# The end of an expert loop: last two passes written out, last expert's rows added on chip, norm by tile

## What is computed

```python
def moe(xn, ...):
    logits = xn @ w_router + b_router
    top_v, top_i = lax.top_k(logits, 4); gates = softmax(top_v)
    # for each expert e, on the rows routed to it:
    hdn = x @ w1[e] + b1[e]
    gate = min(hdn[:, :1024], 7); lin = clip(hdn[:, 1024:], -7, 7)
    y = (gate * sigmoid(1.702 * gate) * (lin + 1)) @ w2[e] + b2[e]
    # each row of y times its gate is added to its token's row
h = h + moe(rmsnorm(h))
out = rmsnorm(h, norm_final_g)
```

## Time and profile before

| | |
|---|---|
| time, median of 3 runs | 2095.84 us (2093.32 to 2096.25) |
| span of the profiled execution | 2096.6 us |
| PE matmul busy | 1978.0 us, 94%, 9222 matmuls |
| DVE busy | 1593.4 us, 76% |
| ACT busy | 1225.3 us, 58% |
| HBM traffic | 260 GB/s over the span |

### The profile page before, as it was taken

The page is one execution under the profiler, slowest core; times in us unless marked ns, Lnnn a source line. Parts: engine busy times, 40 slices in busy tenths (PEclk is TensorE's granted clock), DMA queues, the critical chain, the costliest instruction groups (busy, mean ns, idle before and its releaser), DMA issues. The chain is left out here.

```text
span 2096.6 us, 25970 instructions
## 1 busy us (share of the span) xinstructions
PE 1978.0 (94%) x9222; PEld 1600.6 (76%) x9222; DVE 1593.4 (76%) x1534; ACT 1225.3 (58%) x1058; POOL 245.6 (12%) x177
## 2 busy tenths in 40 slices
PE   6889899999999999999999999999999999999992
PEld 4778677677777888778888888888888888888881
DVE  4753637878775236589999999999999999999983
ACT  5553535446344213357777777777777777777763
POOL 0000031442612000100010010000101000000000
PEclk9899899999999999889999999999999999999996
DMA  5222424442535935489999999999999999999982
GB/s 133 67 77 71 159 73 140 131 140 82 171 97 174 338 99 169 149 320 370 362 374 362 375 363 362 375 367 373 362 375 357 375 360 371 367 358 376 366 298 88
DMA packets 212049, 541.08 MB, mean 258 GB/s; under 512 B 16438, under 2 KB 131544, under 8 KB 175064
## 3 DMA queue, kind: packets, MB, share of 16 engines
q1 hardware_dynamic: 204600, 518.54, 68.0%
q0 software_dynamic: 7392, 21.77, 4.4%
HBM read 512.87 MB, written 31.59 MB: 260 GB/s over the span
## 5 line engine op out<-in xcount | busy, mean ns | idle before, releaser
L1678 DVE TENSOR_TENSOR w_low<-ring_b,w_high 128x2048 fp32r<-128x2048 f32 x192 | 435.8, 2287 | 40.5 <-ACT w_high L1672 40.1
L1678 DVE TENSOR_TENSOR w_low<-ring_a,w_high 128x2048 fp32r<-128x2048 f32 x192 | 435.4, 2286 | 40.3 <-ACT w_high L1672 40.0
L1672 ACT ACTIVATE w_high<-ring_b 128x2048 fp32r<-128x2048 f32 x192 | 368.3, 1919 | 156.7 <-PE ps L1779 109.4
L1672 ACT ACTIVATE w_high<-ring_a 128x2048 fp32r<-128x2048 f32 x192 | 368.1, 1918 | 156.6 <-PE ps L1779 115.0
L1779 PE MATMUL ps<-w_high,rows_high 128*128 128x512 f32 x1024 | 403.7, 394 | 0.2
L1779 PE MATMUL ps<-w_high,rows_low 128*128 128x512 f32 x1024 | 400.4, 391 | 0.0
L1779 PE MATMUL ps<-w_low,rows_high 128*128 128x512 f32 x1024 | 399.5, 390 | 0.0
L1779 PEld LDWEIGHTS ps<-w_high,rows_high 128*128 128x128 f32 x1024 | 193.0, 189 | 42.9 <-DVE w_low L1678 3.5
L1779 PEld LDWEIGHTS ps<-w_high,rows_low 128*128 128x128 f32 x1024 | 192.6, 188 | 41.0
L1779 PEld LDWEIGHTS ps<-w_low,rows_high 128*128 128x128 f32 x1024 | 193.1, 189 | 39.8
L1843 PE MATMUL ps<-w_high,act_high 128*128 128x512 f32 x512 | 207.0, 404 | 15.2 <-DVE w_low L1678 7.6
(11 more groups left out here) (342 smaller groups left out, 2875.2 us busy)
## 6 DMA issues: line engine op xcount, KB each, us to landing
ring_a<-in_w SPq DMA_DIRECT2D x192, 1024.0 KB, 7.8
ring_b<-in_w SPq DMA_DIRECT2D x192, 1024.0 KB, 7.8
unit_raw<-in_w_in SPq DMA_DIRECT2D x80, 512.0 KB, 4.4
temps<-cum_rows SPq DMA_DIRECT2D x16, 1024.0 KB, 7.1
unit_raw<-in_w_up_ssd SPq DMA_DIRECT2D x16, 512.0 KB, 7.9
ssd_out_T<-y_high SPq DMA_DIRECT2D x4, 1024.0 KB, 6.6
ssd_out_T<-y_low SPq DMA_DIRECT2D x4, 1024.0 KB, 6.8
ssd_high<-ssd_out_T SPq DMA_DIRECT2D x4, 1024.0 KB, 11.3
```

Source lines behind the costliest of these rows:

```text
L1672: nc.scalar.activation(w_hi[:, split_at(it, j)], slot(at, 1)[:, 0, :], ACT.Copy).then_inc(w_hi_ok, 1)
L1678: nc.vector.tensor_tensor(w_lo[:, split_at(it, j)], slot(at, 1)[:, 0, :], w_hi[:, split_at(it, j)].bitcast(F32), ALU.subtract).then_inc(w_ ...
```

## The change

The loop ends two passes earlier. Pass 30 is written out with `more=False`: it doesn't prepare later experts (no index matmuls, no `tokens_dve`, no `slots_dve`). Pass 31 is written out as `last_pe`, `last_act`, `last_dve`. It has no row transposes for a next expert. PE instead transposes the 0/1 matrix of expert 31 into bank 6 and ACT copies it to `sel_T`. The transposes of expert 31's activations come before the fourth unit of expert 30's down product. The activations are kept in the buffers of the rows (`rows_hi`, `rows_lo`), and the down product of expert 31 goes to banks 0 and 1.

Expert 31 is not scattered. Its product, times the gate, is split into high and low parts (`y2_hi`, `y2_lo`), and PE multiplies them by `sel_T` into a pair of banks for each tile of tokens. For tiles 0 and 3 PE also adds the residual by a product with the identity; for tiles 1 and 2 DVE adds it. SP reloads the residual once the scatter-add of expert 30 has landed, in the same block of the program; the second block is gone. The norm goes tile by tile: ACT squares and takes the root with scale and bias (a first root on a constant stands ahead of it), DVE takes the reciprocal and does one pass that multiplies by it and by the gain, SP stores each tile. The trip count drops two small DVE instructions, and ACT and POOL one register load each. The cut diff:

```diff
-        def rows_pe(pe, it, odd):
+        def rows_pe(pe, it, odd, more=True):
             pe.wait_ge(xe_in, it * 16 + 16)
-            pe.wait_ge(ix_ok, it * 3 + 6)
+            pe.wait_ge(ix_ok, it * 3 + (6 if more else 3))
...
-                if k == 2:
+                if k == 2 and more:
                     if not is_first(it):
...
-            tokens_dve(v, it + 2)
-            slots_dve(v, it + 3)
+            if more:
+                tokens_dve(v, it + 2)
+                slots_dve(v, it + 3)
...
+        BY_PE = (0, 3)
+        def rows_at(t):
+            return (2 + 2 * t) % 8
...
+        def last_pe(pe, it, end):
+            up_pe(pe, it, 1, False)
+            pe.wait_ge(s_oh, it + 3)
+            pe.wait_ge(a_lo_ok, it)
+            for t in range(NT):
+                last = nc.tensor.transpose(ps[0:CAP, 6, tokens(t)], sel[:, t, :].bitcast(F32), ident[:])
+            last.then_inc(sT_ps, 1)
+            pe.wait_ge(ye_ok, it - 1)
+            for u in range(DOWN):
+                if u == DOWN - 1:
+                    pe.wait_ge(glu_ok, it + 1)
+                    pe.wait_ge(sT_ok, sT_ok0 + 1)
+                    for c in range(NK):
+                        last = nc.tensor.transpose(ps[:, 6 + c // 4, (c % 4) * CAP:(c % 4 + 1) * CAP], l_w[0:CAP, c * P:(c + 1) * P], ident[0:CAP, 0:CAP])
+                    last.then_inc(aT_tp, 1)
+                down_tile(pe, it, UP + u, u, 4, acts_hi, acts_lo).then_inc(w_used, 1)
+            pe.wait_ge(acts2_lo, acts2_lo0 + 1)
+            for u in range(DOWN):
+                down_tile(pe, end, u, u, 0, rows_hi, rows_lo).then_inc(w_used, 1)
+        def last_act(act, it, end, last):
+            for j in range(3):
+                high_act(act, it, 1, j)
+            acts_act(act, it - 1)
+            down_act(act, it - 1, TILES, it * 16 - 32)
+            for j in range(3, UP + 3):
+                high_act(act, it, 1, j)
+            act.wait_ge(h_out, 16 * NT)
+            act.wait_ge(sT_ps, sT_ps0 + 1)
+            nc.scalar.activation(sel_T[0:CAP, :], ps[0:CAP, 6, :], ACT.Copy).then_inc(sT_ok, 1)
+            silu_act(act, it)
+            high_act(act, it, 1, UP + 3)
+            high_act(act, end, 0, 0)
+            act.wait_ge(aT_tp, it + 1)
+            nc.scalar.activation(slots_in(x_hi), eighths(6), ACT.Copy, scale=1.0 / ALPHA).then_inc(acts2_hi, 1)
+            high_act(act, end, 0, 1)
+            down_act(act, it, TILES, last * 16)
+            high_act(act, end, 0, 2)
+            high_act(act, end, 0, 3)
+        def last_dve(v, it, end):
+            for j in range(3):
+                low_dve(v, it, 1, j)
+            acts_dve(v, it - 1)
+            for j in range(3, 6):
+                low_dve(v, it, 1, j)
+            places_dve(v, it - 1)
+            nc.vector.tensor_copy(gate_z2[0:CAP, :], gate_f[0:CAP, bass.ds(it % 4, 1)]).then_inc(last_gate, 1)
+            nc.vector.memset(eps_c, EPS).then_inc(last_gate, 1)
+            v.wait_ge(ix_ps, it + 1)
+            nc.vector.tensor_tensor(sel, iota_r[:, bass.ds(it // NE * CAP, CAP)].unsqueeze(1).broadcast_to([P, NT, CAP]),
+                                    rank_m[:, bass.ds(it % NE * NT, NT)].unsqueeze(2).broadcast_to([P, NT, CAP]), ALU.is_equal).then_inc(s_oh, 1)
+            for j in range(6, UP + 2):
+                low_dve(v, it, 1, j)
+            gate_dve(v, it)
+            low_dve(v, it, 1, UP + 2)
+            linear_dve(v, it)
+            low_dve(v, it, 1, UP + 3)
+            glu_dve(v, it)
+            low_dve(v, end, 0, 0)
+            v.wait_ge(acts2_hi, acts2_hi0 + 1)
+            nc.vector.scalar_tensor_tensor(slots_in(x_lo), eighths(6), 1.0 / ALPHA,
+                                           slots_in(x_hi).bitcast(F32), ALU.mult, ALU.subtract).then_inc(acts2_lo, 1)
+            for j in range(1, DOWN):
+                low_dve(v, end, 0, j)
...
+        def finish_pe(pe):
+            def rows(t, j, part):
+                halves = y2_hi, y2_lo
+                return nc.tensor.matmul(ps[:, rows_at(t) + j, :], sel_T[0:CAP, tokens(t)], halves[part][0:CAP, j * 512:(j + 1) * 512],
+                                        start=part == 0 and t not in BY_PE, stop=part == 1, skip_group_check=True)
+            def residual(t):
+                pe.wait_ge(r_in[t], 48)
+                for j in range(2):
+                    nc.tensor.matmul(ps[:, rows_at(t) + j, :], ident[:], fin[:, t, j * 512:(j + 1) * 512], start=True, stop=False, skip_group_check=True)
+            residual(0)
+            for j in range(2):
+                pe.wait_ge(y2_hi_ok, y2_hi0 + j + 1)
+                for t in range(NT - 1):
+                    rows(t, j, 0)
+            pe.wait_ge(y2_lo_ok, y2_lo0 + 2)
+            for t in range(NT - 1):
+                rows(t, 0, 1)
+                rows(t, 1, 1).then_inc(fin_ps, 1)
+            residual(3)
+            for j in range(2):
+                rows(3, j, 0)
+                last = rows(3, j, 1)
+            last.then_inc(fin_ps, 1)
+        def finish_act(act, end):
+            act.wait_ge(last_gate, last_gate0 + 2)
+            nc.scalar.activation(stat[:, 60:61], eps_c, ACT.Sqrt).then_inc(fin_rt, 1)
+            act.wait_ge(w_used, tile_no(end, DOWN - 1) + 1)
+            for j in range(2):
+                cols = slice(j * 512, (j + 1) * 512)
+                nc.scalar.activation(y2_hi[0:CAP, cols], ps[0:CAP, j, :], ACT.Copy, scale=gate_z2[0:CAP, :]).then_inc(y2_hi_ok, 1)
+            for t in range(NT):
+                if t in BY_PE:
+                    act.wait_ge(fin_ps, fin_ps0 + t + 1)
+                    src = ps[:, rows_at(t):rows_at(t) + 2, :]
+                else:
+                    act.wait_ge(fin_ok, fin_ok0 + t)
+                    src = fin[:, t, :].rearrange("p (a b) -> p a b", a=2)
+                if t:
+                    act.wait_ge(fin_sq, fin_sq0 + t)
+                nc.scalar.activation(fin_junk.rearrange("p (a b) -> p a b", a=2), src, ACT.Square, accum_out=stat[:, t:t + 1]).then_inc(fin_sq, 1)
+                act.wait_ge(fin_sq, fin_sq0 + t + 1)
+                nc.scalar.activation(stat[:, 8 + t:9 + t], stat[:, t:t + 1], ACT.Sqrt, scale=1.0 / D, bias=eps_c).then_inc(fin_rt, 1)
+        def finish_dve(v):
+            v.wait_ge(h_out, 16 * NT)
+            v.wait_ge(gf_in, 48)
+            for j in range(2):
+                cols = slice(j * 512, (j + 1) * 512)
+                v.wait_ge(y2_hi_ok, y2_hi0 + j + 1)
+                nc.vector.scalar_tensor_tensor(y2_lo[0:CAP, cols], ps[0:CAP, j, :], gate_z2[0:CAP, :], y2_hi[0:CAP, cols].bitcast(F32),
+                                               ALU.mult, ALU.subtract).then_inc(y2_lo_ok, 1)
+            for t in range(NT):
+                if t not in BY_PE:
+                    v.wait_ge(fin_ps, fin_ps0 + t + 1)
+                    v.wait_ge(r_in[t], 48)
+                    row = fin[:, t, :].rearrange("p (a b) -> p a b", a=2)
+                    nc.vector.tensor_tensor(row, row, ps[:, rows_at(t):rows_at(t) + 2, :], ALU.add).then_inc(fin_ok, 1)
+            for t in range(NT):
+                v.wait_ge(fin_rt, fin_rt0 + t + 2)
+                nc.vector.reciprocal(stat[:, 12 + t:13 + t], stat[:, 8 + t:9 + t]).then_inc(fin_rc, 1)
+                v.wait_ge(fin_rc, fin_rc0 + t + 1)
+                if t in BY_PE:
+                    v.wait_ge(fin_ps, fin_ps0 + t + 1)
+                    src = ps[:, rows_at(t):rows_at(t) + 2, :]
+                else:
+                    v.wait_ge(fin_sq, fin_sq0 + t + 1)
+                    src = fin[:, t, :].rearrange("p (a b) -> p a b", a=2)
+                nc.vector.scalar_tensor_tensor(fin[:, t, :].rearrange("p (a b) -> p a b", a=2), src, stat[:, 12 + t:13 + t],
+                                               nf_bc.rearrange("p (a b) -> p a b", a=2), ALU.mult, ALU.mult).then_inc(fin_n, 1)
...
             end = after_last(sp)
+            before_end = end - 2
...
+            sp.wait_ge(ye_out, before_end * 16 + 16)
+            for t in range(NT):
+                sp.dma_start(fin[:, t, :], h_d[t * P:(t + 1) * P, :]).then_inc(r_in[t], 16)
+            for t in range(NT):
+                sp.wait_ge(fin_n, t + 1)
+                sp.dma_start(out[t * P:(t + 1) * P, :], fin[:, t, :]).then_inc(f_out, 16)
+            sp.wait_ge(f_out, 32 * NT)
...
-            with pool.Fori(2, end, 2) as pair:
+            with pool.Fori(2, last, 2) as pair:
                 for odd in range(2):
                     scatter_pool(pool, pair + odd - 2)
                     gather_pool(pool, pair + odd + 2, odd)
+            scatter_pool(pool, last - 2)
+            scatter_pool(pool, last - 1)
             scatter_pool(pool, last)
-            scatter_pool(pool, last + 1)
-            pool.wait_ge(xe_in, end * 16 + 32)
-            pool.wait_ge(ye_out, end * 16)
+            pool.wait_ge(xe_in, end * 16)
...
-            down_pe(pe, end, 0)
+            pass_pe(pe, last, 0, False)
+            last_pe(pe, last + 1, end)
```

(62 more changed lines are left out.)

76 lines of the change are left out of this document (13 added, 63 removed).

## The result

The changed kernel takes 2068.16 us, median of four runs (2062.58 to 2072.04), against 2094.63 us (2093.32 to 2096.25) for the kernel before beside it: a ratio of 0.9864, 95% interval 0.9842 to 0.9886. That is 26.5 us less. The profiled execution is the one of 2062.58 us, the shortest of the four.

The account below looks back on a forecast made before the run. PE's matmuls bound the loop, waits and serial chains the tail. 2096.6 - 9.9 (down product) - 15.3 (last matmul to end) = 2071.4; with the median 0.8 us below the span, 2070.6, forecast 2071 us; 8-in-10 range 2066.5 to 2079.

Parts of the forecast that it names:

- Identical head: Code ahead of the tail: taken from one profile with span 2096.6 us, with no bound for its variation.
- the sum's good ends together (4 us): Whole span: favourable bounds of the summed terms, used to set the range's lower end at 2066.5 us.
- 0.8 us below the profiled span: Whole kernel: median of three runs against the profiled span, used to go from 2071.4 to 2070.6 us.
- The last product: Expert 31's down product: last matmul starts at 2054.4 instead of 2064.31, 9.9 us earlier.
- The residual's path: Expert 30's scatter-add and reload: landing at 2052.0 (bounds 2051.1 and 2054.9), first quarter of the residual at 2055.7.
- Rival A: Output products: scatter flies 9.0 us, PE waits for the residual, all later steps shift 2.9 us, 2073.5; chance 0.14.
- Two plain f32 matmuls at 0.44 us: Residual addition on PE: 0.88 us for tile 0, ending at 2056.65; four passes would add 0.95 us.
- The norm: End of kernel: DVE last, from 2061.75 four steps of 1.53 us to 2067.9, then store 3.0 and 0.5 us.
- the 15.3 us: From PE's last down matmul to the end: 32.3 us before, 17.0 after.
- B: Leaving the loop: late code stalls each engine once, up to about 4 us, result 2073 to 2079; chance 0.12.
- C: Code behind the loop: repeated stalls at PE code-block changes, up to 36 us, result 2107, slower than before; chance 0.04.
- D: Tail: expert 31's product still waits and the residual's round trip stays last, within 0.2% or up to 12 us gain; chance 0.06.

Follow-up runs that it names:

- again: The changed kernel measured once more, nothing edited: 2070.23 us, ratio to the kernel before 0.9874.
- old_order: Changed kernel with the last product's earlier order of work: transposes after the fourth unit, evacuation behind three tiles, banks 4 and 5: 2075.98 us, ratio 0.9909.
- early_evac: Kernel before, with ACT evacuating expert 30 ahead of the three high tiles of the last product: 2094.15 us, ratio 0.9996.
- peel: Kernel before with only its last two passes written out complete behind the loop and the new trip count: 2096.53 us, ratio 1.0006.
- one_block: Kernel before with its norm moved into the same program block, instructions and order unchanged: 2091.03 us, ratio 0.9974.
- scatter31_block: Changed kernel with expert 31 scatter-added to HBM and the norm by tile in a second block: 2080.37 us, ratio 0.9919.
- scatter31: Changed kernel with expert 31's rows scatter-added to HBM again, norm by tile in the same block: 2074.98 us, ratio 0.9892.
- late_T: Changed kernel with expert 31's transposes back behind the fourth unit of expert 30's down product: 2073.74 us, ratio 0.9883.
- old_banks: Changed kernel with expert 31's down product back in banks 4 and 5, behind expert 30's evacuation: 2069.3 us, ratio 0.9872.

## Where the prediction was right, and the step that failed

The forecast was 2071 us, the median is 2068.16: the mechanism of the tail was right, and 2071 / 2095.84 = 0.9881 lies in the ratio's interval. The profiled execution, 2062.58, lies below the range, whose lower end was 2066.5. Of the 2.8 us between forecast and median, 1.3 are the gain (25.2 forecast, 26.5 measured), 1.2 the median of before (2095.84, then 2094.63 with the fourth run), the rest rounding. Point by point, in before's clock:

- *Identical head.* The sum took everything up to pass 29 from one profile and gave it no spread. This is the step that failed: the head was 9.2 us shorter in the profiled execution of after, and the four runs of after spread over 9.5 us. The range of the runs of before, 3 us over three runs, was too small a sample (the fifteen beside "again" spread over 10.9 us). Bounds of ±5 us for one execution belong in the range of any change to this kernel. The lower end of 2066.5 rests on "the sum's good ends together (4 us)", but the good ends named are 0.9, 0.3 and 0.5 us, 1.7 in all; with 1.7 us below 2070.6 the range would have begun at 2068.9, above the measured median. That the median lies in the range is thus partly luck.
- *"0.8 us below the profiled span".* This compares different executions. Where the span and the time of one execution are both on record, the time is 1.7 to 1.8 us longer (2060.8 and 2062.58). So before's profile, span 2096.6, would be of an execution of some 2098.4 us (an estimate from 2096.6 and 1.8), longer than all four timed runs of before. That is the same spread of the head again, and the profile that the sum started from stood near its long end.
- *The last product.* 9.9 us expected, 10.2 measured (last down matmul at 2054.10 instead of 2064.31). Expert 30's down product began at 2030.4, 1.4 us earlier than before, where 0.95 had been counted for removed work. The wait before the transposes was to be about 1 us (0.78 measured), the product was to follow without a gap (it did), the clock was to stay at full speed (1.00). old_order gives 8.7 us for this part. Counted from the split of pass 29, its last down matmul is still 1.3 us earlier than before's, since it keeps the work removed from PE's stream. The release read from the earlier trace rows was right; early_evac shows that the evacuation was the last of two waits, not the only one.
- *The residual's path.* Scatter landed at 2051.1 and the first quarter at 2054.7, where 2052.0 and 2055.7 stood: the bound "0.9 us earlier" and not the value taken. Rival A didn't come: the flight was 5.6 us, and PE waited 0.22 us for the landing.
- *Two plain f32 matmuls at 0.44 us.* The mis-sized term of the sum: the rows of PE above show four records for the two calls of `residual(0)`. The first product behind them is recorded from 2046.95 for 0.80 us, where the others take 0.39, so it ends as one that began at 2047.36, 1.83 us after the residual's start. So a call costs 0.91 us, not 0.44 (0.86 us by the same count for `residual(3)`, 2050.10 to 2051.82). All of them, by line (count, then min, median and max ns of one):

```profile
L2026 PE MATMUL ps<-ring_a,ident x8: 590/592/697, 2045.5 to 2051.4; 128*128 128x512 f32 x8
```

  Eight records for the four calls of two tiles. The earlier trace rows was read wrongly in the same way: its eight records are four calls, 3.69 / 4 = 0.92 us each. The Trainium skill, FP8 and Floating Point Precision (TensorE Precision Notes), with its four passes for true FP32, agrees with this: 4 x 0.227 = 0.91. The step that preferred the row to the page had misread the row; the 0.95 us too little were hidden by luck, because the residual came 1.0 us earlier than taken.
- *The norm.* First reciprocal at 2061.3 (2061.75 forecast), DVE last and not ACT, as forecast. The pitch of DVE's chain was 1.39 us, not 1.53: 0.6 us over four tiles. The last store landed in 2.7 us, where 3.0 and 0.5 were taken. Together the end came 15.9 us after the last down matmul instead of 17.0, a gain of 16.4 us where 15.3 stood: 2060.8 + 9.2 = 2070.0, where 2071.4 was the sum.
- *The parts behind the 15.3 us.* The sum subtracted one total from another and never priced the block's end. The runs do: block end 6.7 us (5.6 in the kernel before), rows on chip 6.0, root by tile 3.0; with the order's 8.7 that is 24.4 of 26.7 us. The other 2.3 us were not tried one by one; the work removed from PE's stream and the shorter stores are in them. As old_order shows, the prices depend on the order in which parts are taken away.
- *The rivals.* B and C fell with peel, A and D with the trace of after. The chance of faster, 0.93, rested on the hole and on the 13.2 us from evacuation to reload, and both were gone.

What stays open: why the head's granted clock differs from execution to execution, and how much of the 9.2 us it makes; 1.57 us are seen in one group of matmuls, and thirteen averages that go the same way are no proof for the rest.

## What to carry to other kernels

Before pricing a tail, cut the span at rows that both programs share, and give the part before the cut its own spread, measured over several executions; then compare tails, not times. A hole that ends with one release can have a second just behind it, as here: look for what would be late next, and change the order of all parts together, since here single parts covered for each other. And a block of the program that ends for a few microseconds of norm is worth merging first: here it moved instructions without changing them, for a fifth of the gain. A price read from rows needs the count of calls beside the count of records.

## What the runs showed of the hardware

- A plain f32 matmul of 512 columns is recorded as two records and occupies PE for 0.86 to 0.91 us at the full clock, about four times one of the 0.227 us matmuls around it.
- A block's end between scatter-add and reload makes them 5.8 us (one_block) and 6.0 us (scatter31_block) further apart; the tail is 5.6 and 6.7 us longer.
- The last scatter-add of 96 rows flies 5.1 us (scatter31) to 6.5 us (old_order) when no weights are loaded beside it; the median in after, most of it beside the weights, is 8.9 us.
- In a wait of 7.5 us without matmuls the granted clock went to 0.50 and stayed there for the first 5 us of the product behind it (old_order). Behind a wait of 1.97 us it was at 0.50 for 3 us (late_T); behind one of 1.50 us it stayed at 1.00 (old_banks). The prediction took full speed behind gaps of 1.1 us, and that held in the tail. In the head it differed between executions of the same work: 0.50 and 1.00 in the same eight matmuls, behind the same wait of 1.43 us, which took 3.56 and 1.99 us.
- From the start of the root's table load to the start of the root are 1.29 us, in before (2086.84 to 2088.13) and in after (2038.98 to 2040.27).
